# Four output-projection tiles copied on chip by ScalarE instead of loaded a second time, with norm rows, one row scaling and one square root moved forward

## The reference, cut to what matters

```
mix = einsum('btd,de->bte', g_merge[:, :, 0] * y_a + g_merge[:, :, 1] * y_b, w_out)
h = LN1(alpha * x + mix)                       # ln1_g, ln1_b
q = h @ wq;  s = q . keys                      # 8 heads x 2 halves x 128 keys
sv, si = top_k(s, 16)                          # per half
cand = sv[0][:, None] + sv[1][None, :];  fs, fpos = top_k(cand, 16)
eidx = index of the expert of each of the 16;  g = softmax(fs)
act = gelu(h . u_tab[eidx])
f = sum_k (g * act)[k] * v_tab[eidx[k]]
y = LN2(alpha * h + f)                         # ln2_g, ln2_b
```

## Time and profile before

| | |
|---|---|
| median of 3 executions | 1061.3 us (1059.27 to 1064.37) |
| the profiled execution, its own time | 1062.35 us |
| its span in the trace | 1060.7 us |
| busy: PE / DVE / POOL / ACT | 919.5 / 612.8 / 396.9 / 350.9 us |
| moved by DMA | 389.15 MB, mean 367 GB/s |
| of it the gathers' queue (software_dynamic) | 309.65 MB |
| mean granted TensorE clock | 0.986 of full speed |

### The profile page before, as it was taken

How to read it: one execution, slowest core, us unless ns; L and a number is a source line. 1 busy time by engine, 2 the same in 40 slices (tenths; PEclk the granted TensorE clock), 3 DMA queues, 4 the chain that set the end, 5 groups by cost and what they waited for, 6 DMA issues and landing times.

```text
span 1060.7 us, 14120 instructions
## 1 busy us (share of the span) xinstructions
PE 919.5 (87%) x4011; PEld 529.6 (50%) x4011; DVE 612.8 (58%) x1581; ACT 350.9 (33%) x1099; POOL 396.9 (37%) x448
## 2 busy tenths in 40 slices
PE   8999999899999998899998999877877777777775
PEld 6886566666576854455555545332322222222222
DVE  0001257580022787776866776677886577677664
ACT  1233144321001342544434434433323232432432
POOL 3320222232201433453453554454354454445440
PEclk9999999989999999999999999999999999999999
DMA  8984598879984899999999999999999999999994
GB/s 330 328 311 153 217 320 300 297 292 338 398 317 171 338 420 420 378 412 420 420 420 420 421 421 420 418 415 421 394 407 422 420 422 421 420 415 418 421 393 186
DMA packets 74182, 389.15 MB, mean 367 GB/s; under 512 B 9152, under 2 KB 12296, under 8 KB 40000
## 3 DMA queue, kind: packets, MB, share of 16 engines
q0 software_dynamic: 46320, 309.65, 71.7%
q1 hardware_dynamic: 23144, 72.89, 18.8%
q10 hardware_dynamic: 4656, 5.86, 1.6%
HBM read 385.32 MB, written 7.23 MB: 370 GB/s over the span
## 4 chain that ended last, share of the span: by engine, by line
PE 43%; DMA 33%; DVE 9%; issue 8%; ACT 3%; POOL 2%; SPq 1%; POOLq 1%; DVEq 0%; ACTq 0%
DMA big<-peer_uv,idx_r 28%; PE ps L1365 16%; PE ps L932 8%; PE ps L992 4%; DVE big L1971 4%; DMA ring<-pack_kv 3%; PE ps L1235 3%; PE ps L1198 3%; PE ps L970 3%; POOL big L607 2%; ACT wts L825 1%; PE ps L1220 1%; ACT kv_n L829 1%; PE ps L1173 1%; DMA pg_r<-pack_kv 1%
## 5 line engine op out<-in xcount | busy, mean ns | idle before, releaser
L1365 PE MATMUL ps<-big,kv_n 128*128 128x512 f32 x1024 | 478.1, 611 | 111.3 <-ACT kv_n L829 111.2
L607 POOL DMA_INDIRECT big<-peer_uv,idx_r x264 | 300.4, 1138 | 365.8 <-PE ps L1365 295.6
L1971 DVE CUSTOM_DVE_ANT_0 big<-big,x_n 128x1024 f32<-128x1024 f32 x256 | 311.9, 1226 | 142.6 <-DMA big<-peer_uv,idx_r 138.8
L1365 PEld LDWEIGHTS ps<-big,kv_n 128*128 128x128 f32 x1024 | 187.8, 193 | 365.5 <-issue 190.1
L819 ACT ACTIVATE gel<-dots 128x2 f32<-128x2 f32 x132 | 26.9, 204 | 390.2 <-DVE dots L1971 390.2
L829 ACT ACTIVATE kv_n<-cst,wts 128x128 f32<-128x128 f32 (+1 forms) x264 | 90.8, 391 | 4.3
L932 PE MATMUL ps<-xT_r,ring 128*128 128x264 f32 x368 | 84.7, 395 | 5.1 <-DMA xT_r<-xT 5.1
L932 PEld LDWEIGHTS ps<-xT_r,ring 128*128 128x128 f32 x368 | 71.7, 195 | 17.7 <-DMA ring<-wall 5.1
L1235 PEld LDWEIGHTS ps<-xT_r,ring 128*128 128x128 f32 x512 | 62.0, 191 | 10.2 <-issue 10.2
L825 ACT ACTIVATE wts<-gk,gel 128x1 f32<-128x1 f32 (+1 forms) x256 | 61.7, 287 | 12.7 <-ACT gel L819 0.4
L1235 PE MATMUL ps<-xT_r,ring 128*128 128x128 f32 (+1 forms) x512 | 64.1, 279 | 0.1
(11 more groups left out here) (376 smaller groups left out, 918.8 us busy)
## 6 DMA issues: line engine op xcount, KB each, us to landing
ring<-wall SPq DMA_DIRECT2D x68, 512.0 KB, 7.7
ring<-pack_kv SPq DMA_DIRECT2D x52, 320.0 KB, 5.0
ring<-pack_kv POOLq DMA_DIRECT2D x44, 320.0 KB, 4.7
big<-pack_cmp POOLq DMA_DIRECT2D x42, 128.0 KB, 3.8
pg_r<-pack_kv SPq DMA_DIRECT2D x16, 320.0 KB, 8.6
pg_r<-pack_kv POOLq DMA_DIRECT2D x16, 320.0 KB, 6.7
big<-peer_uv,idx_r POOLq DMA_INDIRECT x264, 11.2
big<-wall SPq DMA_DIRECT2D x2, 2048.0 KB, 12.5
```

The lines of the kernel that those rows point to most:

```text
L607: pool.indirect_dma_start(uv_rows[:, slot, :], None, a["peer_uv"], off).then_inc(uv_in[slot], 16)
L1365: return mm(ps[:, 4 + 2 * tt + c, :], at, row, start=False, stop=stop)
L1971: v.tensor_tensor_reduce(out=uv_rows[:, slot, 0:D], in0=uv_rows[:, slot, 0:D], in1=hrow, scale=1.0, scalar=0.0, op0=ALU.mult, op1=ALU.add, ...
```

## The change

- **Copies.** SP's four loads at L513 go. In their place ACT copies tiles 0 to 3 of `w_out[0]` into the same ring slots (`keep_out(4)` to `keep_out(7)`, 128 x 1024 each) and counts them in the new semaphore `kept_sb`. `other_out(4)` to `other_out(7)` on PE wait for `kept_sb` instead of the ring slot's load. `ring_slots` no longer counts these loads.
- **POOL.** Ahead of gather slot 4 it waits for `kept_sb` to reach 4 (all copies done), where it waited for `out0_mm`.
- **SP.** The four norm vectors are loaded ahead of the first two query tiles, not behind them.
- **DVE.** `alpha_id`, the waits for `ln_in` and `hT_mm`, and `layer_rows(0)` move from behind the second `look_up` to ahead of `find_half(0)`.
- **ACT.** The square root for row tiles 1 and 2 moves from behind `head_group` of group 11 to ahead of it.

```
+            for i, nm in enumerate(("ln1_g", "ln1_b", "ln2_g", "ln2_b")):       # SP
+                sp.dma_start(ln_rows[:, i, :], a[nm].broadcast_to([P, D])).then_inc(ln_in, 16)
             for n in range(W_Q, W_Q + 2):
                 weight(n)
-            for i, nm in enumerate(("ln1_g", "ln1_b", "ln2_g", "ln2_b")):
-                sp.dma_start(ln_rows[:, i, :], a[nm].broadcast_to([P, D])).then_inc(ln_in, 16)
             for n in range(W_Q + 2, W_Q + 4):
                 weight(n)
-            for n in range(W_OUT + 4, W_Q):
-                sp.wait_ge(w_used, W_BEFORE[n] + 1)
-                sp.dma_start(ring[:, W_SLOT[n], :], a["wall"][W_OUT + out_tile(n - W_OUT)]).then_inc(w_in[W_SLOT[n]], 16)
...
                         if zero and slot == 4:                 # POOL
-                            pool.wait_ge(out0_mm, 1)
+                            pool.wait_ge(kept_sb, 4)
...
+            def keep_out(p):                                   # ACT
+                n = W_OUT + p
+                act.wait_ge(w_used, W_BEFORE[n] + 1)
+                nc.scalar.copy(ring[:, W_SLOT[n], :], w_out[0][:, out_tile(p), :]).then_inc(kept_sb, 1)
+
             for n in range(3, 6):
                 other_parts(n)
+            keep_out(4)
             first_features(2)
+            keep_out(5)
             first_features(3)
             expert_exps(1, 0)
+            keep_out(6)
+            keep_out(7)
             first_scores(2)
             first_scores(3)
...
             for g in range(ITEM_HEADS * GROUPS):
+                if g == GROUPS + 3:
+                    act.wait_ge(var_sb, 2)
+                    nc.scalar.sqrt(dev1[:, 0, 1:3], dev1[:, 1, 1:3]).then_inc(std_sb, 1)
                 head_group(0, *divmod(g, GROUPS))
...
-                if g == GROUPS + 3:
-                    act.wait_ge(var_sb, 2)
-                    nc.scalar.sqrt(dev1[:, 0, 1:3], dev1[:, 1, 1:3]).then_inc(std_sb, 1)
...
                 if p >= 4:                                     # PE, other_out
-                    pe.wait_ge(w_in[W_SLOT[w]], 16 * W_LOADS[w])
+                    pe.wait_ge(kept_sb, p - 3)
...
+            own(TS(alpha_id, ident, ALPHA, None, ALU.mult))    # DVE, ahead of find_half
+            dve.wait_ge(ln_in, 64)
+            dve.wait_ge(hT_mm, 1)
+            layer_rows(0)
```

More of the change, by code:

```diff
@@ L134, in ring_slots @@
         last[slot] = n
-        count[slot] = count.get(slot, 0) + 1
+        count[slot] = count.get(slot, 0) + (not W_OUT <= n < W_Q)
         loads.append(count[slot])
@@ L378, in hybrid_layer @@
         ocp_sb, mp_sb = sem("ocp_sb"), sem("mp_sb")
+        kept_sb = sem("kept_sb")
         mgate_sb, mixt_mm, mixt_sb, kev_sb = (sem(n) for n in ("mgate_sb", "mixt_mm", "mixt_sb", "kev_sb"))
@@ L2016, in _ @@
             look_up(8, eidx[:, 0, 8:16], e_sb)
[L2017 to L2020, removed]
             mix_others(0, 1)
```

## The result

The changed kernel takes **1059.28 us** (median of 14 runs, 1056.4 to 1062.23), the kernel before 1061.86 us in the same comparison (14 runs, 1059.27 to 1067.91). The ratio is **0.997, 95% interval 0.9956 to 0.9983**: 3.2 us faster, between 1.8 and 4.7. This is less than the 0.5% that I called distinguishable ahead of time, so it belongs to "within 0.5%", but the interval leaves no change out. The forecast was 5.8 us: right in direction and inside its range, and nearly twice too large.

A forecast was written before the change was run, and what follows sets the result against it. The expert stage was taken as bound by gather bytes at 420 GB/s plus DMA's idle time. Loads -2.5 and dip -3.3 gave -5.8 us, a median from 1061.3 to 1055.5 us; range 1052.5 to 1060.5.

The forecast's parts named there:

- The loads that go: SP's four tile loads: only the last two, among the first gathers, count, 2.5 us; bounds 1.25 and 5.
- thin but positive: DMA work queued ahead of a gather up to group 11: 1.9 us after the change, against 2.5 before.
- The copies, cost 0: Four tile copies on ACT fit into its idle time without delaying slot 4; price 0, bounds 0 and 1 us.
- Row scaling, DVE 2.0 us: Scaling hidden in DVE's wait ahead of the first `max`; first dot from 367.82 to some 365.8 us.
- The square root: ACT's root ahead of group 11: DVE's 4.08 us wait goes; PE's batch of group 12 gains 4 us.
- The dip, 3.3 us: DMA's fall in GB/s from 440 to 455 us closes, and its 3.3 us are recovered at the end.
- (a): Rival at groups 11 and 12: ACT becomes the bound, the dip stays, only loads count; 1059 us, chance 0.16.
- (b): Rival on ACT: a table switch costs twice what the rows show, keeping the dip; 1059.5 us, chance 0.05.
- (c): Rival: all four loads count or a low-clock stretch of later heads goes too; 1053 us, chance 0.13.
- (d): Rival: slower, low-clock stretches at groups 1 to 11 starve DMA's thinner queue; 1062 us and up, chance 0.08.

The follow-up runs named there:

- extra_loads: The changed kernel with eight more unused 512 KB loads issued by SP behind the last query tile's use; 1069.36 us, ratio 1.0047 to the kernel before.
- copies_only: The kernel before with only the four copies on ACT in place of the four loads; ratio 0.9994, stage length 704.8 us.
- before_again: The kernel before itself, unchanged, run and profiled once more; ratio 0.9995, stage length 704.9 us.
- root_only: The kernel before with only the square root moved ahead of group 11; 1061.92 us, ratio 1.0000.
- rows_root: The kernel before with norm vectors, row scaling and square root moved, the four tiles still loaded; ratio 0.9999, stage length 704.5 us.
- rows_only: The kernel before with only the norm vectors and the row scaling moved forward; 1061.48 us, ratio 0.9975.
- late_two_loaded: The changed kernel with the last two of the four tiles (p = 6, 7) loaded by SP again instead of copied; 1060.36 us, ratio 0.9980.

## Why the prediction was right in part

- **The loads that go, 2.5 us: right, with a condition that I did not state.** The landings of the changed kernel are 2.3 to 2.4 us ahead from gather 5 to gather 31, only the last two loads count, and the stage length is 2.5 us shorter in all (704.95 to 702.45). In single executions it can be less: extra_loads, with the same copies, has 1.1 us at both gathers. And copies_only has 2.4 at gather 5 and 0.1 at gather 31. The price holds only because the row scaling moved too; by the queue ahead, "thin but positive", I had made this margin a matter of the dip alone.
- **The copies, cost 0: right.** 1.05 us each (forecast 1.0 to 1.2). PE waits twice from 344 to 366 us, 0.4 and 0.6 us, as before the change. Slot 4 is issued at 359.50 + 1.33 = 360.83 us, before 360.82; slot 6 at 368.56, before 368.57. The estimate by the formula of the Trainium skill ("ScalarE: Activation LUTs", What ACT_TABLE_LOAD costs), 186 ns + 0.833 ns per element, is 1.04 us for 1024 elements; the trace agrees, with 1.05.
- **Row scaling, DVE 2.0 us: right.** It runs from 340.02 to 342.67 us, ahead of the first `max`, which still waits 0.88 us for ACT. The first dot is at 364.31 + 1.33 = 365.64 us (forecast 365.8).
- **The square root: right in each time.** The wait of 4.08 us at `norm_rows` is gone; DVE's dot of group 12 comes after a reciprocal that is 434.66 - 427.10 - 1.33 = 6.2 us earlier (forecast 6). ACT is next late, as said: gelu of group 12 at 432.74 + 1.33 = 434.07 us (forecast 434.3), PE's batch at 434.00 + 1.33 = 435.33 us (435.3), its idle time 0.93 us (about 1), its length 7.13 us instead of 8.83.
- **The dip, 3.3 us: this is the step that failed.** "DMA is never idle and the dip's 3.3 us are recovered. End: -2.5 - 3.3." The first half nearly held (0.5 us of the dip stayed), the second did not follow, for two reasons. The size was read from one execution, in which a low-clock stretch (0.66) fell into the dip; before_again, at a clock of 1.00, lost 2.0 us there (from 80 to 110 us behind the first gather; the first execution lost 3.1 in the same stretch). And a mean of GB/s was taken for a price at the end: what was gained in landings, some 1.7 us, was given back within 25 gathers, between issue and landing. What is left is 0 (root_only, rows_root) to about 1 us (beside the other two parts, where it isn't told from 0). So the sum is 2.5 + 0 to 1 and not 2.5 + 3.3; measured 3.2 us (1.8 to 4.7).
- **The rivals.** (a), ACT becomes the bound and the dip stays at 1059 us, gives the measured time by the wrong cause: ACT was in time and the dip went. (b), double switch costs: the second load starts at 425.85, 0.02 us behind the root's end at 425.83, and the gelu at 427.22, so the 1.28 us are all that a switch costs here. The Trainium skill ("ScalarE: Activation LUTs", What ACT_TABLE_LOAD costs) adds 1.38 us of drain; this trace has no room for it. (c) and (d) did not come; low-clock stretches moved elsewhere (below) and neither starved the early groups nor vanished.

**What stays open** is why the last part of a gather falls behind its bytes at gathers 54 and 74, and with it why the closed dip is handed back; and whether the root is worth nothing or up to 1 us beside copies. A thing that goes with the lead in bytes is seen later: from 291 to 311 us behind the first gather every kernel with the root moved falls to between 391 and 410 GB/s and every one without to between 412 and 421, with PE busy for 19.1 to 19.3 of 20 us in all. For the first 31 gathers the issue times show that compute and bytes hold each other up; behind that no run separates a second limit of that kind from the uneven queue.

## What to carry to other kernels

When two chains are both close to their limit, cost an edit by what each of the two gains: bytes saved where compute is no earlier, or compute moved forward where the bytes are the same, bought 0 to 0.6 us of stage length here (copies_only, rows_only, rows_root), both together some 2.5 us. A fall of mean GB/s in one profiled execution is an upper bound for what filling it brings, not its price: look at it in a second execution, and compare the times at which whole transfers land before and well behind it. To compare profiles of single executions, count from the start of the stage in question; here that took away up to 2.8 us of scatter and left up to 0.7 us between two executions, and 1.5 us where a third could be compared. So an effect of 1 us needs more executions than two.

## What the runs showed of the hardware

- **Mean bandwidth and landings part.** At 420 GB/s in both kernels the finished gathers of root_only lost 2.1 us against those of before_again within 21 gathers (53 to 74), while its bytes stayed 1.4 us ahead. I had taken the two for the same.
- **A low-clock stretch is a matter of the execution.** Before had one at 440 us (0.66), before_again none from 434 to 464 us. The changed kernel has one at 674 us, and behind it DMA runs thin, at 376 GB/s for 15 us, which is 1.6 us:

```profile
674.00:679.00 5.00, 4.04 (x6) 1.75 (x7) 2.54 (x5) 1.21 (x5) 1.44 (x2) 0.70 1.01 422
679.00:694.00 15.00, 15.00 (x34) 5.83 (x33) 10.28 (x29) 8.13 (x21) 7.05 (x7) 0.99 0.99 376
```

- **The first 350 us scatter as much as the change is worth.** The first gather is issued at 355.73 and 354.14 us in two executions of the kernel before, at 354.40 and 356.17 in two of the changed one, at 357.25 and 354.49 in two without the root; over all kernels it lies between 350.63 (late_two_loaded) and 358.47 us (rows_only). How much of this wider spread the kernels themselves make, one execution each doesn't tell.
